# Moving the start of the reused part of SBUF back by 128 bytes

## The chip, the cores and the metric

The kernel runs on one core of a Trainium2 chip. The metric is the device time of one execution in microseconds (us). The core's matrix engine is TensorE (PE in the profile; its weight loads are PEld), beside it work VectorE (DVE), ScalarE (ACT), GpSimd (POOL) and SyncE (SP), whose queue issues every DMA of this kernel. SBUF is the on-chip memory that all of them read; a tile lies at one byte offset, the same in each of 128 partitions.

## The reference

The program computes two transformer-like blocks, one after the other, on x of 1024 tokens by 1024 channels, all in float32:

```python
def reference(x, ...):
    # first block
    h = rms_norm(x, pre_norm_w)
    p = h @ w_in                        # 1024 x 8320, as split below
    y_a = rwkv7_branch(token_shift(p_rwkv, mu), ...)   # 8 heads of 64, a recurrence over the tokens
    y_b = short_conv_branch(p_conv, conv_w)            # 512 channels, window 3
    y_c = pool_branch(p_pool, pool_w, pool_scale)      # 512 channels, windows 2, 4, 8, 16
    gates = sigmoid(p_gate)                            # 3 x 1024
    merged = sum_n gates[n] * (y_n @ w_branch[n])
    x = x + rms_norm(merged @ w_out, post_norm_w)
    # second block
    n = rms_norm_2(x, attn_norm_w)
    proj = n @ w_in_2
    y_attn = windowed_gqa_sink(rope(q), rope(k), v, sink)   # 8 heads, 2 key heads, window 128
    y_ret = silu(rg) * norm(bidirectional_retention(rq, rk, rv, ...))
    h = x + concat(y_attn, y_ret) @ w_out_2
    m = rms_norm_2(h, ffn_norm_w)
    return h + (silu(m @ w_gate) * (m @ w_up)) @ w_down     # inner width 2816
```

## The kernel before, in words

Every large product is made of three products of rounded float32 parts (type float32r): high by high, high by low, low by high. The class `Kernel` lays out SBUF by hand with `Bump`, which hands out byte offsets one after the other, each tile's size rounded up to 32 bytes. There are three parts in a row:

- From `B0`: `Hhi` and `Hlo` (the two parts of the normed activations), and from `BW` three raw weight tiles `Wraw`, four `Whi` and four `Wlo`. All of these begin at a byte offset that is 128 above a multiple of 512.
- From `B1`: the constants `cst` (3,648 bytes; the identity matrix for transposes is its first part), `par` (396 bytes, rounded to 416), `drv` (160), `expo` (64) and `m1_small` (128).
- From `B2` to the end: a part that is used again by every stage with other tiles. The input stage has `xs`, `xn`, `xj`, `g_row` there. The first block's recurrence has `AB`, `WU`, `Zt`, `BK`, `twad`, `wup`, `kb`, `rb`, `RAV`, `Cc`, `kkn_r`, `rk_r`, `kp`, `Nn`, `Tt`, `Yy`, `Yt`, `bones_r`, `cu`, `cy`, `cz` and more. Then come `Mt`, `tg`, `WoHi`, `WoLo`, `Yhi`, `Ylo`, `yst`, `zst` (gates and branch products), `YMhi` and `YMlo` (the second block's mixed activations, later the normed input of the feed-forward part), the tiles of attention and retention, the norms' `xr`, `xo`, `xrb`, `xob`, and `acc`, `fb`, `sgb`, `tgb`, `ot` at the end.

The program is written out engine by engine. Each engine has several streams of steps (Python generators), and a string in `ORDER` says in which order the steps of its streams are woven. TensorE's stream `d` is the dense products (`dense` and `by_token`), and the other letters are the small products of the recurrence, attention and transposes, put between them. Semaphores carry every dependence. Nothing in the order, the waits or the DMAs depends on the value of `B2`.

A dense product of 512 columns is one weight load and one matmul. Its moving operand is `Hhi`/`Hlo`, `Yhi`/`Ylo` or `YMhi`/`YMlo`, with `Whi`/`Wlo` as weights. In `by_token` the moving operand is `WoHi`/`WoLo` (stage D, weights `Hhi`/`Hlo`) or `Hhi`/`Hlo` (stage F, weights `YMhi`/`YMlo`). In the trace's naming, out<-moving,weights. The down projection again moves `Hhi`/`Hlo`. A transpose moves the identity in `cst` and has the tile that is transposed as its weights.

Of the kernel before, what the change touches and what calls it, by code (L numbers as in the profile page):

```python
# [281 lines left out]
class Kernel:  # L282


    def __init__(self, nc, ctx, D, picks):
# [14 lines left out]
        mc = Bump(nc, B1, end)  # L300
# [4 lines left out]
        self.hka, self.oka = drv[:, 25:29], drv[:, 29:33]  # L305
        self.expo = mc("expo", [128, 16])
        self.ss2 = mc("m1_small", [128, 32])
        mc.at += (128 - mc.at) % 512
        B2 = mc.at
        self.PS = ctx.enter_context(nc.psum_tensor("PS", [128, 4096], F32))  # L310
        self.banks = Banks(self.PS, picks)
# [2344 lines left out]
```

How the kernel before makes its waits and increments, by code:

```python
    def wait_ge(self, sig, value):  # L113
        if self.met.get(sig.name, 0) < value:
            self.met[sig.name] = value
            self.h.wait_ge(sig.sem, value)
# [366 lines left out]
    def tokens_in():  # L483
        pe.wait_ge(*S.start_dve.at("zero"))
        for i in range(WARM):
            t = pe.mm(SB[3], K.Whi[NSPL - 1][:, 0, :], K.Whi[NSPL - 1][:])
        t.then_inc(*S.xtr_pe.tick("warm"))
        yield
        for i in range(8):
            for j in range(2):
                bank, before = banks.take(("x", i, j), ("SB0", "SB1", "SB2", "SB3"), [S.xlo_dve.at((i, j))])
                for m in before:
                    pe.wait_ge(*m)
                pe.wait_ge(*S.cst_dma.at("ident"))
                pe.wait_ge(*S.xn_dve.at(i))
                for q in range(4):
                    t = pe.tr(bank[:, q * 128:(q + 1) * 128], K.xn[i % NXN][:, (4 * j + q) * 128:(4 * j + q + 1) * 128], ident)
                t.then_inc(*S.xtr_pe.tick((i, j)))
                yield
# [4 lines left out]
    def dense(tiles, rhs_hi, rhs_lo, ready, parts=FULL, k_outer=False, dps=("DP0", "DP1")):  # L504
# [22 lines left out]
        for ti, n, jj, q, k, part in steps:  # L527
            KTs, name, done = tiles[ti]
            if ti not in bank:
                bank[ti], before = banks.take(("dp", name), dps, done)
                for m in before:
                    pe.wait_ge(*m)
            KT = sum(KTs)
            hi, lo = K.Whi[n % NSPL][:, q, :], K.Wlo[n % NSPL][:, q, :]
            pe.wait_ge(*S.w_act.at(n))
            for m in ready(k, part[0][0], part[-1][1]):
```

## Time and profile before

| what | value |
|---|---|
| median of 3 runs | 2390.61 us |
| lowest and highest of them | 2385.96 and 2390.64 us |
| the profiled execution's own time | 2390.61 us |
| its span, first to last instruction | 2388.5 us |
| around the span | 2.1 us |
| TensorE busy | 98% of the span, 12,848 matmuls |
| VectorE, ScalarE, GpSimd busy | 47%, 29%, 15% |
| DMA traffic | 160.30 MB in 232,698 packets |
| mean granted TensorE clock | 0.993 of full speed |

Busy time of TensorE is modelled and matmuls overlap, so the distance from one matmul's start to the next one's start tells more than its duration. A row of the timeline gives start and length in us, a row of one tile gives minimum/median/maximum duration in ns.

### The profile page before, as it was taken

How to read it: one execution, taken by the hardware profiler on the slowest of the kernel's cores; microseconds unless marked ns; L12 is line 12 of the kernel's file. 1: busy time of each engine (PE TensorE's matmuls, PEld its weight loads, DVE VectorE, ACT ScalarE, POOL GpSimd, SP SyncE). 2: the span in 40 equal slices, each digit the busy share in tenths (PEclk: the TensorE clock that was granted, in tenths of full speed). 3: DMA queues.
4: the chain of work that ended last, by engine and by line, in shares of the span. 5: the costliest groups of instructions: out<-in, count | busy, mean ns of one | idle time of the engine just before them, and what ended most of it. 6: DMA issues, size and time to landing. Idle time of an engine off the chain costs nothing.

```text
span 2388.5 us, 30834 instructions
## 1 busy us (share of the span) xinstructions
PE 2349.4 (98%) x12848; PEld 1933.1 (81%) x12848; DVE 1121.7 (47%) x1981; ACT 696.8 (29%) x1146; POOL 369.7 (15%) x270
## 2 busy tenths in 40 slices
PE   8999999999999999999999999999999999999999
PEld 7888788877878888888887777778888888888887
DVE  4677768778741223164376777543222122222223
ACT  5323233333331212232344444432221212111210
POOL 3312223123100011032121222100101000100100
PEclk9999999999999999999999999899999999999999
DMA  4111211212231312142121111042111111111132
GB/s 146 49 53 49 61 52 45 61 48 70 83 109 49 102 49 96 54 150 82 65 71 45 49 45 49 22 151 80 53 49 49 49 49 49 46 52 49 49 131 72
DMA packets 232698, 160.30 MB, mean 67 GB/s; under 512 B 42608, under 2 KB 216304, under 8 KB 232560
## 3 DMA queue, kind: packets, MB, share of 16 engines
q1 hardware_dynamic: 232560, 158.33, 22.4%
q8 instruction: 102, 1.67, 0.3%
q14 instruction: 36, 0.29, 0.0%
HBM read 127.89 MB, written 23.59 MB: 63 GB/s over the span
## 4 chain that ended last, share of the span: by engine, by line
PE 88%; DVE 8%; POOL 1%; issue 1%; ACT 1%; DMA 1%; SPq 0%; DVEq 0%; ACTq 0%
PE PS L119 85%; PE PS L122 3%; DVE qx L128 1%; DVE Ntmp L128 1%; DVE Nn L128 1%; DVE qr L128 1%; POOL sm L128 0%; DVE smx L1960 0%; DVE ST L136 0%; DVE Yt L136 0%; DMA g_row<-in_pre_norm_w_dram 0%; DVE sm L1772 0%; DVE Yt L128 0%; POOL rsb L128 0%; DVE Wlo L128 0%
## 5 line engine op out<-in xcount | busy, mean ns | idle before, releaser
L119 PE MATMUL PS<-Hhi,Whi 128*128 128x512 f32 (+1 forms) x1792 | 564.3, 390 | 6.4 <-ACT tg L125 3.9
L119 PE MATMUL PS<-Hlo,Whi 128*128 128x512 f32 (+1 forms) x1792 | 565.3, 391 | 0.0
L119 PE MATMUL PS<-Hhi,Wlo 128*128 128x512 f32 (+1 forms) x1792 | 564.9, 391 | 0.0
L125 ACT ACTIVATE Whi<-Wraw 128x512 fp32r<-128x512 f32 x334 | 209.0, 626 | 1089.6 <-PE PS L119 1085.5
L128 DVE TENSOR_TENSOR Wlo<-Wraw,Whi 128x512 fp32r<-128x512 f32 x252 | 179.4, 712 | 620.8 <-ACT Whi L125 620.4
L119 PEld LDWEIGHTS PS<-Hhi,Whi 128*128 128x128 f32 x1792 | 331.8, 189 | 72.8 <-ACT tg L125 4.4
L119 PEld LDWEIGHTS PS<-Hlo,Whi 128*128 128x128 f32 x1792 | 332.1, 189 | 67.7 <-issue 5.4
L119 PEld LDWEIGHTS PS<-Hhi,Wlo 128*128 128x128 f32 x1792 | 331.6, 189 | 67.8 <-issue 4.3
L119 PE MATMUL PS<-YMhi,Whi 128*128 128x512 f32 (+1 forms) x720 | 222.3, 384 | 0.0
L119 PE MATMUL PS<-YMhi,Wlo 128*128 128x512 f32 (+1 forms) x720 | 222.2, 384 | 0.0
L119 PE MATMUL PS<-YMlo,Whi 128*128 128x512 f32 (+1 forms) x720 | 222.1, 384 | 0.0
L128 POOL TENSOR_TENSOR Wlo<-Wraw,Whi 128x512 fp32r<-128x512 f32 x82 | 127.6, 1557 | 390.4 <-ACT Whi L125 390.3
L119 PEld LDWEIGHTS PS<-YMlo,Whi 128*128 128x128 f32 x720 | 135.3, 188 | 26.8
L119 PEld LDWEIGHTS PS<-YMhi,Wlo 128*128 128x128 f32 x720 | 135.3, 188 | 26.8
L119 PEld LDWEIGHTS PS<-YMhi,Whi 128*128 128x128 f32 x720 | 135.2, 188 | 26.8
L128 POOL TENSOR_TENSOR Hlo<-fb,Hhi 128x1024 fp32r<-128x1024 f32 x22 | 52.6, 2392 | 592.3 <-ACT Hhi L125 592.3
L128 DVE TENSOR_TENSOR Ntmp<-Nn 32x30 f32<-32x30 f32 (+14 forms) x240 | 90.2, 376 | 36.9 <-DMA Nn<-scr_ns 30.8
L128 DVE TENSOR_TENSOR Nn<-Nn,Ntmp 32x30 f32<-32x30 f32 (+14 forms) x240 | 92.6, 386 | 6.6
L125 ACT ACTIVATE smx<-smx,small 128x385 f32<-128x385 f32 (+3 forms) x96 | 55.4, 583 | 52.4 <-DVE small L132 30.2
L136 DVE SCALAR_TENSOR_TENSOR fb<-sgb,PS 128x1024 f32<-128x1024 f32 x22 | 26.9, 1221 | 84.5 <-PE PS L119 84.5
L119 PE MATMUL PS<-Yhi,Whi 128*128 128x512 f32 x192 | 59.2, 390 | 1.2 <-DVE Ylo L128 1.2
L119 PE MATMUL PS<-Ylo,Whi 128*128 128x512 f32 x192 | 59.2, 389 | 0.0
(291 smaller groups left out, 2719.2 us busy)
## 6 DMA issues: line engine op xcount, KB each, us to landing
Wraw<-in_w_in_dram SPq DMA_DIRECT2D x166, 256.0 KB, 2.8
Wraw<-in_w_gate_dram SPq DMA_DIRECT2D x44, 256.0 KB, 2.9
Wraw<-in_w_up_dram SPq DMA_DIRECT2D x44, 256.0 KB, 2.8
Wraw<-in_w_down_dram SPq DMA_DIRECT2D x32, 256.0 KB, 2.8
Wraw<-in_w_branch_dram SPq DMA_DIRECT2D x24, 256.0 KB, 2.8
yst<-scr_y SPq DMA_DIRECT2D x12, 512.0 KB, 3.8
xs<-in_x_dram SPq DMA_DIRECT2D x8, 512.0 KB, 6.8
scr_y<-cy SPq DMA_DIRECT2D x8, 512.0 KB, 2.6
```

The lines of the kernel that those rows point to most:

```text
L119: return self.h.matmul(out, lhsT, rhs, start=start, stop=stop, skip_group_check=True)
L122: return self.h.transpose(out, in_, ident)
L125: return self.h.activation(out, in_, func, **kw)
L128: return self.h.tensor_tensor(out, a, b, op)
L136: return self.h.scalar_tensor_tensor(out, a, s, b, op0, op1)
```

## The change

```diff
@@ -305,7 +305,7 @@
         self.expo = mc("expo", [128, 16])
         self.ss2 = mc("m1_small", [128, 32])
-        mc.at += (128 - mc.at) % 512
+        mc.at += -mc.at % 128
         B2 = mc.at
```

The line pads the end of the constants before the reused part of SBUF starts at `B2`. Before, `B2` is the next offset that is 128 above a multiple of 512. After, it is the next multiple of 128.

## Rows read from the trace of the kernel before

**Rows 1.** The page's first lines: span, and busy time, share, instructions of each engine.

```profile
span 2388.5 us, 30834 instructions
PE 2349.4 (98%) x12848; PEld 1933.1 (81%) x12848; DVE 1121.7 (47%) x1981; ACT 696.8 (29%) x1146; POOL 369.7 (15%) x270
```

**Rows 2.** The page's chain that ended last, by engine.

```profile
PE 88%; DVE 8%; POOL 1%; issue 1%; ACT 1%; DMA 1%; SPq 0%; DVEq 0%; ACTq 0%
```

**Rows 3.** Groups of TensorE by tile and form: xcount | busy us, mean ns.

```profile
L119 PE MATMUL PS<-YMhi,Whi 128*128 128x512 f32 x688 | 213.2, 389 | 0.0
L119 PE MATMUL PS<-Yhi,Wlo 128*128 128x512 f32 x192 | 59.1, 389 | 0.0
...
L119 PE MATMUL PS<-WoHi,Hlo 128*128 128x512 f32 x128 | 39.6, 390 | 0.0
L119 PE MATMUL PS<-Hlo,YMhi 128*128 128x512 f32 x128 | 39.5, 390 | 0.0
...
L119 PE MATMUL PS<-YMlo,Whi 128*128 128x256 f32 x32 | 9.1, 283 | 0.0
...
L119 PE MATMUL PS<-rk_r,bones_r 128*128 128x512 f32 x8 | 3.2, 394 | 0.0
L119 PE MATMUL PS<-kkn_r,bones_r 128*128 128x512 f32 x8 | 3.1, 390 | 0.0
```

**Rows 4.** Timeline of TensorE: start us, length us, in the feed-forward stage.

```profile
1656.81 0.39 PE L119 MATMUL PS<-YMhi,Whi 128*128 128x512 f32 x1
...
1662.48 0.39 PE L119 MATMUL PS<-YMlo,Whi 128*128 128x512 f32 x1
...
1668.97 0.28 PE L119 MATMUL PS<-YMhi,Whi 128*128 128x256 f32 x1
...
1674.73 0.28 PE L119 MATMUL PS<-YMhi,Whi 128*128 128x256 f32 x1
```

**Rows 5.** Tiles as a transpose's weights: kp, kr, xr; duration ns min/median/max.

```profile
L122 PEld LDWEIGHTS PS<-cst,kp x32: 137/140/143, 61.0 to 548.1; 128*128 128x128 f32 x32
...
L122 PEld LDWEIGHTS PS<-cst,kr x32: 137/140/143, 1221.3 to 1464.6; 128*128 128x128 f32 x32
...
L122 PEld LDWEIGHTS PS<-cst,xr x64: 138/140/143, 1102.8 to 1168.3; 128*128 128x128 f32 x64
```

**Rows 6.** Tiles written by VectorE and ScalarE: cy, acc, vrt, YMhi; duration ns min/median/max.

```profile
L128 DVE TENSOR_TENSOR cy<-PS,cy x4: 1205/1225/1226, 115.2 to 404.7; 128x1024 f32<-128x1024 f32 x4
...
L128 DVE TENSOR_TENSOR acc<-PS,acc x17: 691/1225/1225, 2081.6 to 2383.5; 128x1024 f32<-128x1024 f32 x15, 128x512 f32<-128x512 f32 x2
...
L125 ACT ACTIVATE vrt<-PS x8: 572/588/601, 1223.9 to 1460.6; 128x512 f32<-128x512 f32 x8
...
L125 ACT ACTIVATE YMhi<-PS x24: 574/597/599, 1284.8 to 1664.1; 128x512 fp32r<-128x512 f32 x24
```

**Rows 7.** DMA issues: xcount, KB each, median us from issue to landing.

```profile
scr_y<-cy SPq DMA_DIRECT2D x8, 512.0 KB, 2.6
...
scr_x<-xob SPq DMA_DIRECT2D x8, 512.0 KB, 2.6
...
wup<-in_wup_dram SPq DMA_DIRECT2D x1, 256.0 KB, 5.4
pw<-in_pool_w_dram SPq DMA_DIRECT2D x1, 256.0 KB, 5.8
```

**Rows 8.** The critical chain's first entry and the timeline's last DMA.

```profile
3.32 7.92 DMA g_row<-in_pre_norm_w_dram
...
2385.73 0.37 SPq L145 DMA_DIRECT2D out_dram<-ot  x1
```

**Rows 9.** One window: us, then busy us of each engine, PEclk, DMA share, GB/s.

```profile
1500.00:1600.00 100.00, 93.37 (x485) 73.74 (x484) 48.83 (x84) 37.79 (x66) 4.21 (x6) 0.91 0.27 80
```

## The prediction

> **What bounds the kernel now.** I read the page's busy times first, then the chain that ended last, then TensorE's groups and its timeline, and last the rows of single tiles and the DMAs. TensorE is busy for 98% of the span, and the next engine, VectorE, for 47% [rows 1]. The chain has 88% on TensorE, 8% on VectorE and 1% on DMAs [rows 2]. So this is one engine's stream of matmuls, and what counts is the step from one start to the next. In the feed-forward stage 25 steps of 512 columns take 1662.48 - 1656.81 = 5.67 us, 0.227 us each; 48 steps of 256 columns take 1674.73 - 1668.97 = 5.76 us, 0.120 us each [rows 4]. The reader is to see that the 256 further columns cost 0.107 us, which is one column per cycle at 2.4 GHz, and that 0.227 - 2 x 0.107 = 0.013 us are left, whatever the length. Neither a wait nor the memory's rate sets the step, unless these 13 ns hide something of the operands' addresses.
>
> **What the change does.** I add up the layout. The allocator's first free byte in this program is 16,481, so `B0` is 16,512, which is 32 x 512 + 128. 65,536 bytes of activations and 11 x 2,048 of weights bring `B1` to 104,576. The constants take 3,648 + 416 + 160 + 64 + 128 = 4,416 bytes, up to 108,992. Before, this is padded by 192 to 109,184 (128 above a multiple of 512); after, by 64 to 109,056, which is 213 x 512. So every tile from `B2` on moves down by 128 bytes, and nothing else changes: no instruction, wait, DMA or order. The tiles that began 128 above a multiple of 512 (`YMhi`, `Yhi`, `WoHi`, `acc`, `xr`, `ot`, most of them) now begin at a multiple of 512. Those of the recurrence go from 256 to 128 (`twad` to `Cc`), from 288 to 160 (`kkn` to `bones_r`), from 64 to 448 (`cy`, `cz`); `kr` goes from 192 to 64. `Hhi`, `Whi`, `Wraw` and `cst` stay. A shift of 128 leaves every offset as it was modulo 128; only an effect of a coarser grain, of 256 or 512 bytes, can come of it. No copy or buffer is gained by the 128 bytes.
>
> **TensorE.** The 512-column matmuls whose moving operand moves: 3 groups of 688 with `YM`, 3 of 192 with `Y`, 3 of 128 with `Wo` [rows 3], where one of each three stands, together 2,064 + 576 + 384 = 3,024, and 3 x 32 = 96 of 256 columns: 3,120. Stage F has 3 x 128 = 384 more whose weights move. So 3,504 of 12,848 touch a moved operand. The trace of before has no large matmul at a multiple of 512, so I bound the cost by the nearest rows. For weights, the row of 128 columns is 140 ns for `kp` (offset 288 modulo 512), 140 for `kr` (192) and 140 for `xr` (128) [rows 5]: no dependence, and in each of them the identity lies in `cst` at 128, so the two operands' distance modulo 512 was 160, 64 and 0 without a difference. For the moving operand I have `kkn_r` and `rk_r` at 288, with a mean of 390 and 394 ns against 389 for `YMhi` and `Yhi` [rows 3], which bounds a loss by 1 to 5 ns each; these two stand alone between matmuls of other kinds, which can explain it as well. A gain is bounded by the 13 ns above. I take 0, since the columns run at one per cycle and the weights show no dependence. Term: 0, bounds -3,120 x 13.3 ns = -41.5 us and +3,504 x 5 ns = +17.5 us.
>
> **VectorE, ScalarE, GpSimd.** An addition of 1024 columns is 1,225 ns into `cy` (offset 64) and 1,225 into `acc` (128); a copy of 512 columns from PSUM is 588 ns into `vrt` (192) and 597 into `YMhi` (128), with overlapping extremes [rows 6]. I take 0. If it were 9 ns for each of VectorE's 1,981 instructions, it would be 17.8 us on that engine; 8% of the chain is on it [rows 2], so 1.4 us would reach the end, of either sign. The rest lies beside TensorE's work.
>
> **DMAs.** The weight loads into `Wraw`, most of the traffic, are not moved, and are prefetched behind TensorE. Of the others, 512 KB out of `cy` (64) and out of `xob` (128) both land after 2.6 us [rows 7]. Into `wup`, the one transfer to an offset that was a multiple of 256, 256 KB take 5.4 us, against 5.8 for `pw` (64) in the same start-up burst: 7% at most. DMAs are 1% of the chain, 24 us; 7% of that is 1.7 us, and I take a third of it, -0.6 us, since the clean pair shows nothing. The places are `g_row`, on which the first VectorE work waits for 7.92 us, and the last store, issued at 2385.73 [rows 8]. `AB`'s 128-byte pieces exchange places between the two DMAs that carry them and give nothing.
>
> The Trainium skill, DMA: Bandwidth & Descriptors, section "How a descriptor splits into AXI transactions", says that a transfer has to begin its first transaction at the 256-byte boundary below its start, so that an unaligned one fetches bytes for nothing; by it 4,096 bytes that begin 128 past a boundary cost 132 beats and not 128, 3%, and the sum would have -0.7 us here in the place of my -0.6. This trace has no pair of rows that shows it.
>
> **Sum.** The profiled execution took 2390.6 us, 2388.5 of span and 2.1 around it, the same as the median of the runs: 2390.6 + 0 + 0 - 0.6 = 2390.0 us. The three runs lie 4.7 us apart (2385.96 to 2390.64) with nothing changed. One place where such a difference arises is the stretch from 1500 to 1600, where TensorE idles for 6.6 us and has a mean clock of 0.91 [rows 9]: a stretch at the lower level is shorter or longer with what came just before it.
>
> **The rivals.**
> *Nothing can be measured* (my forecast): 2385 to 2395 us, the runs' own spread to either side.
> *TensorE gets faster.* The 13 ns of each step would be the price of moving operands that begin 128 past a multiple of 512, and go away for 3,120 matmuls: 2390.6 - 41.5 = 2349 us; half of it gives 2370. For it: every large moving operand of before begins at 128, so the trace can't exclude it, and a fixed price per matmul is what a badly placed start would look like. Against it: `kkn_r`, at another place in the 512 bytes, is not faster but 1 ns slower. Chance 0.07. The Trainium skill, TensorE: Matmul & The Clock Gate, section "Wait — 56ns, not 53.3ns?", has a step of 215.7 ns for 512 columns at the full clock, in bf16; this trace has 227, so by that page 11 ns of the 13 would be to be had, and the time would be 2356 us if the address were their cause.
> *TensorE gets slower* (the other side). The moving operand and the weights, now both at 128 modulo 512 in every dense product, come to stand at different places, and one operand's fetch meets the other's: 1 to 5 ns for each of 3,504 matmuls [rows 3], +3.5 to +17.5 us, 2394 to 2408. It decides from 1.4 ns per matmul on (4.8 us / 3,504). For it: `kkn_r` and `rk_r` are the slowest of their form. Against it: the three transposes at distances 160, 64 and 0 are equal. Chance 0.13.
> *The transfers matter more than their chain share*, in the two stages with most of them (the start and the norms): all 24 us of DMA in the chain by 20% would be -5 us, 2386. Chance 0.05.
> *The pad changes nothing at all*, if the end of the constants already stood at both paddings' offset. It doesn't, by the sum above (192 against 64).
>
> **How the numbers follow.** No measurable effect has 0.75, faster by the matrix step 0.07, slower by it 0.13, DMAs 0.05. What this kernel's measurement can tell from no change is 0.2%, 4.8 us. Of the no-effect case, some 0.03 falls on either side of that by the spread of the runs. Faster: 0.07 + 0.04 + 0.03 = 0.14. Slower: 0.13 x 0.8 (the rest of that rival lies under 1.4 ns) + 0.03, about 0.14. Same: 0.72. The likeliest is 2390.0. The range goes from the lowest run with 2 us below it, 2384, to 2398, which takes in the lower half of the slower rival; outside are the matrix gain and that rival's upper half.
>
> **What would show it.** In the profile after, the step of 512 columns with `YM` as moving operand: 0.227 us and 0.120 us for 256 means the first step is right; 0.214 to 0.22 is the faster rival, 0.229 and more the slower one, and then `Hhi` with `Whi` should keep 0.227, since neither is moved. Additions of 1024 columns should stay at 1,225 ns, weight loads at 140. Landing times of `scr_x<-xob` and `xr` should stay within 0.1 us. The prediction is wrong if a shift of place below 512 bytes is seen by any engine, or if a small change of one transfer's time moves the waits of the woven order.

## The result: 20 us slower, and the profile after

| | before | after |
|---|---|---|
| median | 2390.62 us (4 runs, 2385.96 to 2391.24) | 2410.49 us (4 runs, 2407.56 to 2410.83) |
| profiled execution, its span | 2390.61, 2388.5 us | 2412.46, 2410.3 us |
| mean granted TensorE clock | 0.993 | 0.993 |

The ratio is 1.0085, with a 95% interval from 1.0067 to 1.0102. The kernel after is slower by 0.85%, outside the predicted range (2384 to 2398), and on the side to which 0.14 was given.

The page's first lines of the kernel after answer to [rows 1], and its chain by engine to [rows 2].

```profile
span 2410.3 us, 30834 instructions
PE 2370.0 (98%) x12848; PEld 1934.6 (80%) x12848; DVE 1122.0 (47%) x1981; ACT 696.4 (29%) x1146; POOL 369.5 (15%) x270
PE 88%; DVE 8%; POOL 1%; issue 1%; ACT 1%; DMA 1%; SPq 0%; DVEq 0%; ACTq 0%
```

The reader is to see that the span grew by 21.8 us and TensorE's busy time by 20.6 (2370.0 - 2349.4), with as many instructions. The three other engines are within 0.4 us of before, and the chain's shares are the same. So no large new wait has come: the matmuls themselves cost more. Which ones is seen in TensorE's groups by tile and form, kernel after (xcount | busy us, mean ns of one | idle before), against [rows 3]:

```profile
L119 PE MATMUL PS<-Hhi,Whi 128*128 128x512 f32 x1696 | 536.5, 396 | 5.5 <-ACT tg L125 3.9 <-DVE qb L136 1.4 <-DVE twad L136 0.2
L119 PE MATMUL PS<-YMhi,Whi 128*128 128x512 f32 x688 | 217.6, 395 | 0.0
L119 PE MATMUL PS<-Yhi,Wlo 128*128 128x512 f32 x192 | 60.4, 395 | 0.0
L119 PE MATMUL PS<-WoHi,Hlo 128*128 128x512 f32 x128 | 40.3, 395 | 0.0
L119 PE MATMUL PS<-Hlo,YMhi 128*128 128x512 f32 x128 | 40.1, 395 | 0.0
```

`YMhi,Whi` went from 213.2 us to 217.6, `Yhi,Wlo` from 59.1 to 60.4, `WoHi,Hlo` from 39.6 to 40.3, `Hlo,YMhi` (its weights moved) from 39.5 to 40.1. `Hhi,Whi`, of which neither operand moved, has 536.5 us now, and had 536.2 before:

```profile
L119 PE MATMUL PS<-Hhi,Whi 128*128 128x512 f32 x1696 | 536.2, 396 | 5.1 <-ACT tg L125 3.9 <-DVE qb L136 0.9 <-DVE twad L136 0.2
```

The step itself is in the timeline of the feed-forward stage (start us, length us), which answers to [rows 4]:

```profile
1665.80 0.40 PE L119 MATMUL PS<-YMhi,Whi 128*128 128x512 f32 x1
...
1671.63 0.39 PE L119 MATMUL PS<-YMlo,Whi 128*128 128x512 f32 x1
...
1678.20 0.28 PE L119 MATMUL PS<-YMhi,Whi 128*128 128x256 f32 x1
...
1683.96 0.28 PE L119 MATMUL PS<-YMhi,Whi 128*128 128x256 f32 x1
```

25 steps of 512 columns took 5.67 us and take 5.83, so 0.2268 us became 0.2332; 48 steps of 256 columns took 5.76 us and take 5.76. Only the long ones pay. The same in windows, first the two of before (from and to in us, width, then busy us and count of PE, PEld, DVE, ACT, POOL, then PEclk, DMA share, GB/s). In the first window of each pair `YM` is the moving operand, in the second `Hhi` and `Hlo`:

```profile
1700.00:1780.00 80.00, 80.00 (x355) 66.24 (x354) 18.66 (x23) 17.39 (x23) 9.56 (x4) 1.00 0.17 48
1870.00:1900.00 30.00, 30.00 (x134) 24.84 (x133) 4.15 (x6) 6.54 (x9) 0.00 (x0) 1.00 0.15 44
```

and after:

```profile
1700.00:1780.00 80.00, 80.00 (x346) 64.82 (x346) 19.17 (x23) 16.33 (x22) 7.21 (x3) 1.00 0.16 46
1870.00:1900.00 30.00, 30.00 (x134) 24.82 (x133) 3.46 (x5) 4.99 (x7) 0.00 (x0) 1.00 0.18 53
```

PE shows 80.00 of 80 us busy in both, at full clock in both. Busy time can't show the loss here, since a slower matmul is just as busy; the count does: 346 matmuls where there were 355. With `H` as moving operand it is 134 both times.

Last, where in the program the 21.8 us lie. These rows of single tiles give minimum/median/maximum ns and then the first and last start; first before:

```profile
L119 PE MATMUL PS<-Yhi,Whi x192: 389/389/497, 702.9 to 1062.3; 128*128 128x512 f32 x192
L119 PE MATMUL PS<-WoHi,Hhi x128: 387/389/497, 1063.4 to 1155.9; 128*128 128x512 f32 x128
L119 PE MATMUL PS<-Hhi,YMhi x128: 387/389/500, 1560.8 to 1655.7; 128*128 128x512 f32 x128
L119 PE MATMUL PS<-YMhi,Whi x720: 278/389/473, 1656.8 to 2299.2; 128*128 128x512 f32 x172, 128*128 128x256 f32 x8
```

and after:

```profile
L119 PE MATMUL PS<-Yhi,Whi x192: 387/395/501, 703.5 to 1066.7; 128*128 128x512 f32 x192
L119 PE MATMUL PS<-WoHi,Hhi x128: 390/393/502, 1067.9 to 1162.3; 128*128 128x512 f32 x128
L119 PE MATMUL PS<-Hhi,YMhi x128: 387/392/502, 1567.9 to 1664.6; 128*128 128x512 f32 x128
L119 PE MATMUL PS<-YMhi,Whi x720: 283/392/478, 1665.8 to 2321.2; 128*128 128x512 f32 x172, 128*128 128x256 f32 x8
```

After is late by 0.6 us where `Y` starts, 4.4 where it ends (+3.8 for 576 matmuls), 6.4 at the last `WoHi,Hhi` (about +2), 7.1 at the first `Hhi,YMhi` (+0.7 in attention), 8.9 at its last (+1.8 for 384), and 22.0 at the last `YMhi,Whi` (13.1 since, for 2,064 matmuls of `YM`). 13.1 / 2,064 is 6.3 ns for each. All but 1.3 of these 22.0 us are in the matmuls that touch a moved tile; the span's end is 21.8 us late.

### The profile page after: what moved, and what is told of

Read it like the earlier page. It is cut to its first block, busy times and chain, and to the rows that moved or that the text cites. A ratio compares the mean times of both kernels' runs of the same rounds, so it can differ in the third digit from the quotient of the medians.

```text
span 2410.3 us, 30834 instructions
## 1 busy us (share of the span) xinstructions
PE 2370.0 (98%) x12848; PEld 1934.6 (80%) x12848; DVE 1122.0 (47%) x1981; ACT 696.4 (29%) x1146; POOL 369.5 (15%) x270
## 4 chain that ended last, share of the span: by engine, by line
PE 88%; DVE 8%; POOL 1%; issue 1%; ACT 1%; DMA 1%; SPq 0%; DVEq 0%; ACTq 0%
PE PS L119 85%; PE PS L122 3%; DVE qx L128 1%; DVE Ntmp L128 1%; DVE Nn L128 1%; DVE qr L128 1%; POOL sm L128 0%; DVE smx L1960 0%; DMA g_row<-in_pre_norm_w_dram 0%; DVE ST L136 0%; DVE Yt L136 0%; DVE sm L1772 0%; DVE Yt L128 0%; POOL rsb L128 0%; DVE Cc L1636 0%
## 5 line engine op out<-in xcount | busy, mean ns | idle before, releaser
L119 PE MATMUL PS<-YMhi,Whi 128*128 128x512 f32 (+1 forms) x720 | 226.7, 390 | 0.0
L119 PE MATMUL PS<-Yhi,Whi 128*128 128x512 f32 x192 | 60.4, 395 | 1.1 <-DVE Ylo L128 1.1
L119 PE MATMUL PS<-Yhi,Wlo 128*128 128x512 f32 x192 | 60.4, 395 | 0.0
```

The source lines that it names most:

```text
L119: return self.h.matmul(out, lhsT, rhs, start=start, stop=stop, skip_group_check=True)
```

## The experiments

What is to be told apart is *why* these matmuls are slow. The distance theory: they are slow because moving operand and weights no longer start at the same offset. The distance is the moving operand's start less the weights' start, in bytes. The place theory: they are slow because an operand starts at a multiple of 512 (or 256), wherever the other one lies.

### Steps by themselves: each operand at many places (m1_steps)

```diff
+# moving operand's start and the weights' start, modulo 512; columns
+SETS = [(m, 128, 512) for m in range(0, 512, 32)]
+SETS += [(m, w, 512) for w in (0, 256, 384) for m in (0, 128, 256, 384)]
+SETS += [(0, 128, 256), (128, 128, 256), (0, 128, 512), (128, 128, 512)]
...
+for m, w, cols in SETS:
+    for i in range(N):
+        h = i % 2
+        t = e.matmul(PS[:, 512 * h:512 * h + cols], wt[w][:, (i // 2) % 4, :], mv[m][:, 512 * h:512 * h + cols], start=True, stop=True, skip_group_check=True)
```

> A kernel that computes nothing of the reference and only measures: 48 matmuls per group, 512 columns of float32r, each with its own weight load, the start of the moving operand at one of sixteen offsets modulo 512 (32 apart) with the weights at 128, then a grid of 0, 128, 256, 384 for both. It leaves the whole reference out. Distance theory (a step is longer where the two operands' starts differ modulo 512): 227 ns where moving and weights have the same offset, about 233 elsewhere, so four of the sixteen cells of the grid are fast, on the diagonal. Place theory (a step is longer where one of the operands begins at a multiple of 512): about 233 in the row and the column of 0, 227 in the nine other cells. If neither, all groups alike at 227: then the address acts only together with what the other engines do. With 256 columns, offset 0 against 128: 126 against 120 if the surplus is one fixed price per matmul, 123 if it grows with the columns.

The three kernels that only measure (m1, m2, m3) were run once each, at a granted clock of 1.00; a step is the mean of 48 matmuls. TensorE's timeline of this one, one row for 48 matmuls; the third letter of a tile is its place (a 0, e 128, i 256, m 384 modulo 512; b to p in steps of 32), `mv` the moving operand, `wt` the weights:

```profile
83.00 11.05 PE L57 MATMUL PS<-mve,wte 128*128 128x512 f32 x48
93.89 11.37 PE L57 MATMUL PS<-mvf,wte 128*128 128x512 f32 x48
105.09 11.16 PE L57 MATMUL PS<-mvg,wte 128*128 128x512 f32 x48
...
216.42 11.05 PE L57 MATMUL PS<-mva,wta 128*128 128x512 f32 x48
227.31 11.35 PE L57 MATMUL PS<-mve,wta 128*128 128x512 f32 x48
238.50 11.06 PE L57 MATMUL PS<-mvi,wta 128*128 128x512 f32 x48
...
348.94 5.92 PE L57 MATMUL PS<-mva,wte 128*128 128x256 f32 x48
354.70 5.92 PE L57 MATMUL PS<-mve,wte 128*128 128x256 f32 x48
```

A step is the distance to the next row's start by 48: `mve,wte` (93.89 - 83.00) / 48 = 226.9 ns, `mvf,wte` (105.09 - 93.89) / 48 = 233.3. A row's length tells as much: 11.05 is fast, 11.35 slow, and `mvg,wte`, 64 above the weights, with 11.16 between them (229 ns). With weights at 0, the moving operand at 0 and at 256 is fast (11.05, 11.06), at 128 slow (11.35). So 128 apart is slow whichever of the two is at 0, and two operands at 0 are fast: place falls, distance stands, and it counts modulo 256. Of the 16 pairs of 0, 128, 256 and 384, the 8 whose difference is a multiple of 256 are fast and the 8 others slow. 64 above the weights costs a third of it. 256 columns have a row of 5.92 us at either distance, a step of 120.0 ns: neither of the two prices that I had in mind for it. Pairs that were measured twice agree within 1 ns: `mva,wte` 233.1 and 232.5 ns.

### The kernel with all large operands at a multiple of 512 (e1_all0)

```diff
+def LAYOUT(base):
+    B1 = base
+    B0 = B1 + 4416
+    B0 += (0 - B0) % 512
+    BW = B0 + 65536
+    return B0, BW + (0 - BW) % 512, B1
...
-        B0, BW, B1 = base, base + 65536, base + 65536 + 2048 * (NRAW + 2 * NSPL)
+        B0, BW, B1 = LAYOUT(base)
...
-        mc.at += -mc.at % 128
+        mc.at = mw.at + (0 - mw.at) % 512
```

The constants come first and stay 128 above a multiple of 512; `H`, `W` and the reused part start at a multiple of 512.

> All of it begins at multiples of 512: the constants come first, then the activations H at 0, the weight tiles W at 0, the reused part at 0. Distance theory: every dense product again has moving operand and weights at the same offset, steps 227 ns everywhere, about 2390 us as the kernel before. Place theory: 6.3 ns more for all 8,544 matmuls of 512 columns, +54 us, about 2444 us.

Measured: 2391.05 us (10 runs) against 2392.58 for before on the same chip (13 runs), ratio 0.9993 [0.9983, 1.0004]. Its window with `YM`:

```profile
1700.00:1780.00 80.00, 80.00 (x355) 66.24 (x354) 19.43 (x23) 17.08 (x23) 9.56 (x4) 1.00 0.17 50
```

355 again: `YM`, `Y` and `Wo`, which the change had moved to 0, are still at 0, and the price is gone since `Whi` and `Hhi` are at 0 too.

### The price moved to other matmuls (e2_w0)

Now `H` stays at 128, and the weights are at 0 together with the reused part.

```diff
+def LAYOUT(base):
+    B0 = base
+    B1 = B0 + 65536
+    BW = B1 + 4416
+    return B0, BW + (0 - BW) % 512, B1
...
-        B0, BW, B1 = base, base + 65536, base + 65536 + 2048 * (NRAW + 2 * NSPL)
+        B0, BW, B1 = LAYOUT(base)
...
-        mc.at += -mc.at % 128
+        mc.at = mw.at + (0 - mw.at) % 512
```

> The reused part at 0 as in the changed kernel, and the weight tiles W moved to 0 as well; H stays at 128. Distance theory: YM and Y with W go back to 227 ns, H with W rises to 233 (5,088 matmuls x 6.3 = +32 us), the two stages by token stay slow (768 x 6 = +4.6 us): about 2427 us. Place theory: YM, Y and H with W all at 233: about 2444 us.

Measured: 2414.90 us (4 runs), ratio 1.0098 [1.0079, 1.0117]. The two windows, the page's line of TensorE and one group of this kernel:

```profile
1700.00:1780.00 80.00, 80.00 (x354) 66.24 (x353) 19.77 (x24) 16.93 (x23) 9.61 (x4) 1.00 0.19 55
1870.00:1900.00 30.00, 30.00 (x130) 24.11 (x130) 3.50 (x6) 5.90 (x8) 0.00 (x0) 1.00 0.17 50
```

```profile
PE 2378.4 (99%) x12848; PEld 1936.1 (80%) x12848; DVE 1122.2 (46%) x1981; ACT 696.6 (29%) x1146; POOL 367.1 (15%) x270
L119 PE MATMUL PS<-Hhi,Whi 128*128 128x512 f32 x1696 | 545.3, 401 | 5.1 <-ACT tg L125 3.9 <-DVE qb L136 0.9 <-DVE twad L136 0.3
```

The picture of after is turned over: `YM` is fast (354), `H` slow (130 for 134), as are the `Wo` and stage F groups, in which `H` at 128 meets a tile at 0, and `Hhi,Whi` rose from 536.2 to 545.3 us although `H` stands where it always did. The three groups of `H` with `W` rose by 27.0 us together, 5.3 ns for each of 5,088. That is less than the 6.3 ns apiece that I had counted on, and many of these matmuls have the small ones of the recurrence or of attention between them. In the traces, those among them that stand ten or more behind the last small matmul step at 226.7 ns before and 232.9 here, 6.2 more; the first nine behind it step at 230.0 before and 233.4 here, 3.4 more. A second part is lost in waits: TensorE's busy time rose by 29.0 us (2378.4 - 2349.4) and the span by 25.5 (2414.0 - 2388.5). The direction was as the distance theory says, and my size was 12 us too large.

### The reused part at 256 (e3_b256)

```diff
-        mc.at += -mc.at % 128
+        mc.at += (256 - mc.at) % 512
```

> The kernel before with the reused part at 256 modulo 512, the same distance of 128 from W and H as in the changed kernel, upwards. Distance theory: YM, Y, Wo and stage F at about 233 ns, about 2411 us, as the changed kernel. Place theory: no operand at a multiple of 512, 227 ns, about 2390 us.

Measured: 2412.82 us (4 runs), ratio 1.0092 [1.0069, 1.0115], and 346 matmuls in the window from 1700 to 1780, as after. A multiple of 256 against 128 is as dear as a multiple of 512.

### The layout of after, with its large tiles back at 128 (e4_r128)

```diff
-        R1, R2 = B2, B2 + 65536
+        R1, R2 = B2 + 128, B2 + 128 + 65536
```

This leaves the input's and the recurrence's tiles where after has them, and puts `WoHi`, `Yhi`, `YMhi`, attention's and the norms' tiles back.

> The changed kernel, with its parts R1 and R2 (Wo, Y, YM, the tiles of both norms, attention, retention and the feed-forward stage) put back 128 bytes up; only the tiles of the input stage and of the recurrence stay moved. Distance theory: all 3,504 matmuls of 512 columns that had lost their common offset have it again, steps 227 ns, within 1 us of the kernel before, near 2391 us. If the shift cost something in the recurrence or in the transfers too, some of the 20 us stays: above 2396 us.

Measured: 2391.85 us (11 runs) against 2390.05 (21 runs), ratio 1.0004 [0.9995, 1.0013]. The whole loss is in the tiles from `R1` on. The shift of the recurrence's tiles and of the input's costs nothing that can be measured: the interval allows some 3 us.

### Another residue that should be fast (e5_all0_b256)

```diff
         # on top of e1_all0
-        mc.at = mw.at + (0 - mw.at) % 512
+        mc.at = mw.at + (256 - mw.at) % 512
```

> H and W at 0, the reused part at 256 modulo 512. Distance modulo 512: YM, Y and Wo with a partner at another offset, about 2411 us, steps 233 ns. Distance modulo 256, as the first measuring kernel has it (moving operand at 256 and at 384 with partners at 0 and 128: 227 ns): steps 227 ns, as the kernel before, near 2391 us.

Measured: 2390.96 us (10 runs), ratio 1.0001 [0.9992, 1.0010], 355 matmuls in the window. A start at 256 is as good as one at 0 if the weights are at 0, though it was dear with weights at 128 (e3_b256): in the kernel too the distance counts modulo 256.

### 64 bytes apart (e6_b192 and e7_b448)

```diff
-        mc.at += -mc.at % 128
+        mc.at += (192 - mc.at) % 512      # e7_b448: (448 - mc.at) % 512
```

> The kernel before with the reused part 64 bytes up, at 192. The measuring kernel has 228.8 ns for the moving operand 64 bytes above the weights and 233.3 for 64 below. So Wo, Y and YM as moving operand (3,024 matmuls) should take 228.8 ns, +2.2 each = +6.6 us, and stage F, where the weights are moved (384), 233, +2.5 us: about 2400 us. A theory in which any difference costs the same gives 2411 us.

> The kernel before with the reused part at 448 modulo 512, that is 192 bytes down from the weights' and H's offset. If only the distance modulo 256 counts, this is the run at 192 once more (192 down is 64 up): steps near 229 ns with Wo, Y and YM moving, 233 in stage F, about 2401 us. If sign or size count otherwise, up to 2412 us.

Measured: 2401.17 us, ratio 1.0047 [1.0032, 1.0062], and 2402.62 us, ratio 1.0055 [1.0038, 1.0072], 4 runs each. Two rows of e6_b192:

```profile
1700.00:1780.00 80.00, 80.00 (x351) 65.62 (x351) 18.57 (x22) 16.47 (x22) 9.72 (x4) 1.00 0.16 47
```

```profile
L119 PE MATMUL PS<-Hlo,YMhi 128*128 128x512 f32 x128 | 40.2, 395 | 0.0
```

With `YM` moving, 64 above the weights, 351 matmuls fit, 4 fewer than before, where after has 9 fewer. In stage F it is `YM` that is the weights, so the moving `Hlo` is 64 *below* them, and these have the full price, a mean of 395 ns as after (390 before). The sign counts. e7_b448 gives the same steps from a place 256 higher.

### Which pairs, which lengths, which types (m2_pairs)

Two theories of what meets what: the matmul's operand collides with the *next* matmul's weight load, or with something of its *own* pair. Tiles that alternate between 0 and 128 tell them apart. The same kernel has shorter matmuls, and bf16.

```diff
+# start modulo 512 of the one or two tiles of a name (two: in turns)
+MOV = {"md": (128,), "mp": (0,), "mx": (0, 128), "bd": (128,), "bp": (0,)}
+WTS = {"wd": (128,), "wp": (0,), "wx": (0, 128), "wy": (128, 0), "vd": (128,)}
```

> Only measures, leaves the whole reference out. Groups of 48 matmuls. First 256, 288, 320, 384, 448, 512 columns with both operands at 128 (md, wd), then the same with the moving operand at 0 (mp, wd): it shows from which length on the distance costs. Then a moving operand whose tile begins at 128 and that is read from its column 32 on, so from 256: 480 columns slow if the start of what is read counts, fast if the tile's. Then pairs in which both tiles alternate between 0 and 128: mx, wx, each matmul's own weights at its moving operand's offset and the next one's weights not; mp, wp, both at 0; mx, wy, the other way about. If the cost comes of the next weights being fetched while the moving operand streams, mx, wx is slow (233) and mx, wy fast (227); if of a matmul's own pair, the other way; if both are between, neither. Last three groups in bfloat16 with both at 128, moving at 0, both at 128: the sizes in bytes are half, and the surplus may be gone.

TensorE's timeline of this kernel, 48 matmuls a row:

```profile
147.85 11.12 PE L64 MATMUL PS<-mx,wx 128*128 128x512 f32 x48
158.81 11.07 PE L64 MATMUL PS<-mp,wp 128*128 128x512 f32 x48
169.72 11.21 PE L64 MATMUL PS<-mx,wy 128*128 128x512 f32 x48
180.77 11.07 PE L64 MATMUL PS<-md,wd 128*128 128x512 f32 x48
191.68 11.36 PE L64 MATMUL PS<-md,wx 128*128 128x512 f32 x48
202.87 11.20 PE L64 MATMUL PS<-mx,wd 128*128 128x512 f32 x48
```

Own pair equal and next weights 128 off (`mx,wx`): 228.3 ns. Own pair off and next equal (`mx,wy`): 230.2. Both theories had one of the two at 226.7 and the other at 233, so neither is right as it stands. Alternating weights under a moving operand that stays (`md,wx`) give 233.1, the full price; an alternating operand over weights that stay (`mx,wd`) has a row as long as that of `mx,wy`, about 230. What the places of the matmuls before do with it was not tried.

One length of the same kernel, groups by form (mean ns of one, of which the differences count; `md` at the weights' offset, `mp` 128 off):

```profile
L64 PE MATMUL PS<-md,wd 128*128 128x448 f32 x48 | 10.1, 368 | 0.0
L64 PE MATMUL PS<-mp,wd 128*128 128x448 f32 x48 | 10.0, 366 | 0.0
```

Steps at equal offsets and 128 off, from the starts in the trace, to 0.2 ns: 256 columns 120.0 and 120.0 ns, 288 131.7 and 133.3, 320 146.7 and 146.7, 384 173.3 and 176.0, 448 206.7 and 203.8, 512 227.1 and 232.4. At 448 columns the sign is the other way. The group of 480 columns, read from 128 bytes into a tile that starts at the weights' offset, settles nothing, since no other group has 480 columns; m3_scan reads into the tile too and answers its question. In bf16 the step, from start to start within a row, is 215.8 ns at either offset. The Trainium skill (TensorE: Matmul & The Clock Gate, "Wait — 56ns, not 53.3ns?") has 215.7 for it, with which this agrees; the 226.7 of float32r is not that figure with a misplaced operand, since no placement reached less.

### The distance in fine steps (m3_scan)

```diff
+# bytes from the weights' start (128 modulo 512) to the moving operand's, modulo 256
+UP = (0, 4, 8, 16, 32, 48, 64, 80, 96, 112, 128, 144, 160, 176, 192, 208, 224, 240, 252, 0)
...
+MOV.update({"fd": (128,), "fp": (0,)})
+# weights 64 below and 64 above
+WTS = {"wd": (128,), "wu": (64,), "wv": (192,), "gd": (128,)}
```

> Only measures, leaves the whole reference out. Groups of 48 matmuls of 512 columns with the weights at 128; the moving operand is read from 0, 4, 8, 16, 32, 48, 64, ... 240, 252 bytes further on (da to ds, then da again). If any difference counts, only da has 227 ns and 4 bytes already cost 5 to 7 ns; if it is a matter of lines or of 32-byte pieces, the first few groups (4, 8, 16) stay at 227. Then the moving operand back at 128 and the weights 64 bytes below it and 64 above it (wu, wv): if only the difference counts, as 64 up and 64 down of the moving operand in the first measuring kernel, about 229 and 233. [...]

TensorE's timeline, in which `da` to `ds` are these distances in order, and `fd`, `fp` and `gd` are plain float32:

```profile
45.23 11.04 PE L67 MATMUL PS<-da,wd 128*128 128x512 f32 x48
56.11 11.53 PE L67 MATMUL PS<-db,wd 128*128 128x512 f32 x48
...
234.93 11.05 PE L67 MATMUL PS<-dr,wd 128*128 128x512 f32 x48
245.82 11.19 PE L67 MATMUL PS<-ds,wd 128*128 128x512 f32 x48
...
267.73 11.15 PE L67 MATMUL PS<-da,wu 128*128 128x512 f32 x48
278.71 11.36 PE L67 MATMUL PS<-da,wv 128*128 128x512 f32 x48
...
300.82 41.36 PE L67 MATMUL PS<-fd,gd 128*128 128x512 f32 x96
```

0 bytes 226.7 ns, 4 bytes (`db`) 236.7, the dearest of all, 8 bytes 231.5, 16 bytes 231.7, then 228.8 to 234.6 up to 224 bytes (64 is that 228.8), 240 bytes 226.9, 252 bytes 229.8. All the moving tiles start at the weights' offset and are read from further on, so what counts is where the reading starts. Weights 64 below (`wu`) give 228.8 and 64 above (`wv`) 233.3, as e6_b192 has in its two stages. Plain float32 takes 429.2 ns at distance 0, and the row for 128 off is as long.

## Why the prediction was wrong

**What bounds the kernel** was right: TensorE's steps set the end, and 6.3 ns of each matmul reached the span almost in full. The 13 ns left over by two 256-column halves did not hide a price of the address that could be taken away: no placement gave less than 226.7 ns. But a price could be put on top of it.

**What the change does** was right, offsets included. The sentence that only a grain of 256 or 512 bytes could show holds for this shift: the price repeats every 256 bytes. Within the 256 it depends on every few bytes (m3_scan).

**TensorE** is the step that failed. I took 0 for the term, with bounds of -41.5 and +17.5 us. It is 3.8 + 2 + 1.8 + 13.1 = 20.7 us, above the upper bound, as much as TensorE's busy time grew (20.6), and 6.1 ns for each of the 3,408 matmuls of 512 columns (the 96 of 256 columns pay nothing). The other 1.3 us are the 0.6 of the start and 0.7 in attention. The rows behind the bound did not vary the quantity at issue:

- `kkn_r` and `rk_r` stood at 288, but so did their weights `bones_r`: distance 0, like every large product. After, the three stand at 160 together and cost what they did; one of their groups, kernel after:

```profile
L119 PE MATMUL PS<-kkn_r,bones_r 128*128 128x512 f32 x8 | 3.1, 392 | 0.0
```

- The transposes did differ in distance (160, 64, 0), but they are 128 columns long and plain float32 [rows 5], and m1_steps and m3_scan find no price at 256 columns nor in plain float32. I had also read their weight loads, where the price is in the step of the matmul.
- So no row of before bore on two float32r operands of 512 columns that start at different offsets. An absence of rows was taken for evidence of no effect.

**The slower rival** had the mechanism, in its words "come to stand at different places", and the groups (`YM`, `Y`, `Wo`, stage F) that show it; its chance was 0.13 and its size 1 to 5 ns, where 6.3 were measured with `YM`: its time, 2394 to 2408, ends 2.5 us short of the result. Its signature was named in advance: 0.229 or more for `YM`, and `Hhi` with `Whi` unchanged. That one operand's fetch meets the other's, its second half, is not shown: m2_pairs contradicts the two plain forms of it, and what happens inside TensorE stays open. The Trainium skill (SBUF — State Buffer, "Who interferes with whom") has the ports for the moving operand and for weight loads as independent. Read so, it speaks against two fetches that meet. No run here shows where the price arises; they show that there is one, 233 against 226.7 ns for float32r.

**The faster rival** is refuted: e1_all0 has every large operand at a multiple of 512, and is 0.9993 of before [0.9983, 1.0004].

**VectorE, ScalarE, GpSimd** at 0 was right: busy 1122.0, 696.4 and 369.5 us, against 1121.7, 696.8 and 369.7.

**DMAs** at -0.6 us: right in being small. `out_dram<-ot` lands earlier after; its row of the DMA issues, whose median was 2.6 us before, and the chain's entry for `g_row` (start, us), which answers to [rows 8]:

```profile
out_dram<-ot SPq DMA_DIRECT2D x16, 256.0 KB, 2.3
```

```profile
3.31 8.78 DMA g_row<-in_pre_norm_w_dram
```

The store gains 0.1 us at the end. `g_row` took 0.86 us longer, enough for the 0.6 us by which `Y` starts late; among the runs of this study it took 7.40 to 8.78 us with no relation to its place, so I read it as spread. `scr_x<-xob` stayed at 2.6. Of the rival of larger DMA effects nothing is seen: it had the time fall by 5 us.

## What to carry to other kernels

Where float32r products of 512 columns, each with its own weight load, fill TensorE, the moving operand and the weights should start at the same offset modulo 256; a pad that looks arbitrary may keep just that, and its residue should be compared with that of the tiles it is multiplied with before it is trimmed. When a cost is bounded by the nearest rows, ask first whether those rows differ in the quantity that the change alters: rows that all share one value bound nothing, and then the range has to stay wide. And where an engine is busy all the time before and after, count its instructions in a window of fixed length, since busy time can't show that each has become slower.

## What the runs showed of the hardware

- A float32r matmul of 512 columns with a weight load of its own takes 226.7 ns from start to start if the two operands start a multiple of 256 bytes apart (or 240 bytes), and 229 to 237 if not. It depends on the signed difference: the moving operand 64 bytes above the weights costs 2 ns, 64 below 6.6. 4 bytes are the worst, 10 ns.
- At a distance of 128 the steps of `YM` in the trace of after are not equal. From 1665.8 to 1671.6 us they take turns, 237 or 238 and 229 or 230 ns; from 1700 to 1780 they repeat a pattern of 7 (241, 233, 231, 231, 229, 230, 232 ns). The means differ a little, 233.2 and 232.4 ns. In before the steps of `YM` are 226 and 227 ns, two of 227 after each 226. What picks the pattern is not known.
- At a distance of 128 the price depends on length and type: none at 256 and 320 columns, 1.6 ns at 288, 2.7 at 384, a gain of 2.9 ns at 448; none at 512 columns in bf16 (215.8 ns) and in plain float32 (429.2 ns). No theory here explains this.
- A store of 256 KB out of `ot` in pieces of 512 bytes lands after a median of 2.3 us where `ot` starts at a multiple of 256 (after, e1_all0, e2_w0, e3_b256, e5_all0_b256) and 2.6 us where it starts at 128, 192 or 448 (before, e4_r128, e6_b192, e7_b448). The 512 KB out of `xob` in pieces of 4,096 bytes land after 2.57 us in the first five and 2.60 in the other four. The direction agrees with what the Trainium skill (DMA: Bandwidth & Descriptors, "How a descriptor splits into AXI transactions") says of transfers that start off a multiple of 256 bytes. One place in the kernel waits for the store, for 0.1 us.
